# Fourteen of the last sixteen rows of v added by TensorE in two banks of its own, behind the first half's layers

## The reference

```
act = gelu(einsum("chkd,cd->chk", take(u, idx), xc))
out = einsum("chk,chkd->cd", act * gates, take(v, idx))
```

## Time and profile before

| | us |
|---|---|
| median of 3 runs | 2494.62 (2493.06 to 2494.7) |
| the profiled execution | 2490.55 |
| its span | 2488.8, so 1.75 outside |
| TensorE busy | 2112.2 (85%) |
| VectorE busy | 1832.5 (74%) |
| ScalarE busy | 1179.3 (47%) |
| GpSimd busy | 757.1 (30%) |
| gathers (q0) | 536.90 MB, 53.0% of the 16 engines' span |
| weights and stores (q1) | 222.15 MB, 23.5% |

### The profile page before, as it was taken

One profiled execution on the slowest core, in us unless ns is written; L12 is line 12 of the kernel. 1 busy time (PEld: TensorE's weight loads), 2 busy tenths in 40 slices (PEclk: granted clock), 3 DMA queues, 4 the chain that ended last, 5 costly groups with the idle time before them and its releaser, 6 DMA issues.

```text
span 2488.8 us, 28611 instructions
## 1 busy us (share of the span) xinstructions
PE 2112.2 (85%) x9508; PEld 1497.4 (60%) x9508; DVE 1832.5 (74%) x3372; ACT 1179.3 (47%) x3776; POOL 757.1 (30%) x634
## 2 busy tenths in 40 slices
PE   6987898988777777999675578699949999998999
PEld 6965443433222225884343466488429978898997
DVE  6985676868888887887898977776575646656564
ACT  5214555555666664442455654433244435435443
POOL 0001444454555553232465643333320001100000
PEclk9988899999999998999785689899969999999999
DMA  5111999999999999999998999999975543224453
GB/s 212 69 68 70 387 403 413 416 417 421 421 421 420 412 418 346 386 421 397 380 416 342 375 414 365 380 411 420 388 319 185 187 176 140 73 98 148 174 187 135
DMA packets 107460, 760.89 MB, mean 306 GB/s; under 512 B 12064, under 2 KB 12832, under 8 KB 16432
## 3 DMA queue, kind: packets, MB, share of 16 engines
q0 software_dynamic: 73728, 536.90, 53.0%
q1 hardware_dynamic: 33584, 222.15, 23.5%
HBM read 756.91 MB, written 2.10 MB: 305 GB/s over the span
## 4 chain that ended last, share of the span: by engine, by line
PE 42%; DVE 9%; DMA 4%; issue 3%; ACT 2%; POOL 1%; DVEq 0%; ACTq 0%; POOLq 0%
PE bank L578 42%; DVE resid L1039 4%; DMA pair<-in_uv,idx 4%; DVE pair L1695 2%; DVE half L1033 1%; DVE tmp L1033 0%; PE bank L996 0%; ACT half L1780 0%; POOL smalls L2328 0%; DVE smalls L1354 0%; POOL pair L2379 0%; ACT sigB L1780 0%; PE bank L870 0%; DVE smalls L1440 0%; ACT frow L1780 0%
## 5 line engine op out<-in xcount | busy, mean ns | idle before, releaser
L2379 POOL DMA_INDIRECT pair<-in_uv,idx x512 | 646.7, 1263 | 882.5 <-DVE resid L1039 552.9
L1780 ACT ACTIVATE smalls<-smalls 128x1 f32<-128x1 f32 x2058 | 540.3, 286 | 661.3 <-DVE smalls L1695 643.2
L1695 DVE CUSTOM_DVE_ANT_0 pair<-pair,hn 128x1024 f32<-128x1024 f32 x512 | 623.7, 1219 | 159.2 <-DMA pair<-in_uv,idx 157.4
L578 PE MATMUL bank<-pair,diag 128*128 128x512 f32 x928 | 457.1, 624 | 122.4 <-ACT diag L1780 121.8
L578 PEld LDWEIGHTS bank<-pair,diag 128*128 128x128 f32 x928 | 167.9, 194 | 392.3 <-ACT diag L1780 247.0
L578 PE MATMUL bank<-ft,raw 128*128 128x256 f32 x1664 | 373.1, 387 | 11.9 <-DVE ft L1033 11.9
L1039 DVE SCALAR_TENSOR_TENSOR resid<-pair,smalls,resid 128x1024 f32<-128x1024 f32 x280 | 358.1, 1279 | 0.9 <-DVE resid L1039 0.5
L578 PEld LDWEIGHTS bank<-ft,raw 128*128 128x128 f32 x1664 | 323.1, 195 | 57.7 <-issue 12.5
L1033 DVE TENSOR_TENSOR half<-raw,half 128x1024 fp32r<-128x1024 f32 (+1 forms) x204 | 235.5, 1194 | 136.0 <-ACT half L1780 136.0
L578 PE MATMUL bank<-ft_hi,half 128*128 128x256 f32 x1664 | 305.9, 285 | 7.4 <-DVE ft_lo L1033 4.1
L578 PEld LDWEIGHTS bank<-ft_hi,half 128*128 128x128 f32 x1664 | 260.8, 191 | 8.3 <-DVE ft_lo L1033 4.3
(11 more groups left out here) (280 smaller groups left out, 2743.0 us busy)
## 6 DMA issues: line engine op xcount, KB each, us to landing
raw<-in_wts SPq DMA_DIRECT2D x196, 1024.0 KB, 6.2
pair<-in_uv,idx POOLq DMA_INDIRECT x512, 11.1
raw<-in_wts SPq DMA_DIRECT2D x10, 512.0 KB, 6.1
raw<-in_wts SPq DMA_DIRECT2D x4, 720.0 KB, 6.9
resid<-in_x SPq DMA_DIRECT2D x4, 512.0 KB, 6.1
out<-resid SPq DMA_DIRECT2D x8, 256.0 KB, 6.0
raw<-in_wts SPq DMA_DIRECT2D x2, 768.0 KB, 6.4
rowt<-in_rows SPq DMA_DIRECT2D x1, 1076.0 KB, 12.3
```

The costliest lines, as they stand in the source:

```text
L578: return e.matmul(o, a, b, start=start, stop=stop)
L1695: e.tensor_tensor_reduce(b[:, 0:1024], b[:, 0:1024], HN[i // 128], 1.0, 0.0, ALU.mult, ALU.add, actv[:, i % 8:i % 8 + 1]).then_inc(dotted, 1)
L1780: return e.activation(o, i, f, **kw)
L2379: e.indirect_dma_start(pair[i % NPAIR], None, uv, bass.IndirectOffsetOnAxis(ap=idx[:, n % SLOTS, k:k + 1], axis=0)).then_inc(pairs_in[i % ...
```

## The change

`ON_PE` becomes true for rows 496 to 509 too. Their matmuls are not in TensorE's loop over rows, which now ends at 496: they stand between chain A and chain B, after the transposes of tile 2, which are taken out of chain B and put ahead of them (`tiles=(0,)`), while those of tile 3 stay in it. They use two mix banks of their own (4 and 5, a fourth mix use that the plan gets after chain A's last FFN), and eight `late_diag` tiles instead of `diag`, in space that chain A has left by then. VectorE leaves out the fourteen adds, takes the banks over after the last dot (`mixed_in(3, PAIRS - 2)`) with a wait on its own two writes, and then adds rows 510 and 511 as before. GpSimd's and ScalarE's waits by `row_used` turn from `added` to `v_used` for the fourteen rows by themselves.

```diff
--- before.py
+++ after.py
@@ -112,7 +112,8 @@
 
 
 
-ON_PE = [i < HALF + 8 and not (i < 128 and i % 4 == 3) for i in range(PAIRS)]
+LAST_ON_PE = 496
+ON_PE = [i < HALF + 8 and not (i < 128 and i % 4 == 3) or LAST_ON_PE <= i < PAIRS - 2 for i in range(PAIRS)]
 
 ROUTES, SLOTS = [], 16
 for _k in [1] * 8 + [2] * 8 + [1, 2, 1, 2, 1] + [0] * 11:
@@ -219,6 +220,8 @@
         for stage, n, us in (("br", 16, 1.8), ("wo", 4, 7.0)):
             p.ring(stage + x, n, us)
         ffn(2)
+        if x == "A":
+            p.add("mix", [4, 5], told=False)
     return p
 
 
@@ -466,6 +469,7 @@
         assert MISC + 512 + 1024 <= CHAIN and PAIR + 6144 <= LOW
 
         FTS = {"1": [FT2[0], ar("ft_early", LAYER + 10752, 8 * HALF, R).rearrange("p (k t) -> p k t", k=8)], "m": FT2, "2": FT2}
+        late_diag = [ar(f"late_diag{i}", LAYER + 12800 + P * i, P) for i in range(8)]
         nearly = [ar(f"nearly{i}", LAYER + 9728 + 512 * i, 512) for i in range(2)]
         rate_on = [rowt[:, P * i:P * i + P] for i in range(2)]
         RATE = {"1": rowt[:, HALF:2 * HALF], "2": rowt[:, HALF:2 * HALF], "m": ar("rate_m", LAYER + 14080, HALF)}
@@ -742,10 +746,10 @@
                     if begun:
                         fresh("mix", 2 * t + h)
                     b = B["mix", 2 * t + h]
-                    ins = mm(bank[b.bank][:], diag[i % 8], pair[i % NPAIR][:, 1024 + h * 512:1536 + h * 512], begun, done)
+                    ins = mm(bank[b.bank][:], (diag if i < LAST_ON_PE else late_diag)[i % 8], pair[i % NPAIR][:, 1024 + h * 512:1536 + h * 512], begun, done)
                 ins.then_inc(v_used, 1)
 
-            for i in range(PAIRS):
+            for i in range(LAST_ON_PE):
                 if i % 16 == 0:
                     steps = scores_in_steps(i // 16 + 2) if i < 128 else iter(())
                 if ON_PE[i]:
@@ -802,10 +806,10 @@
                 for n in range(4):
                     taken(e, "norm" + k if k[0] != "m" else "norm_" + k, n)
 
-            def turned_unscaled(k, from_):
+            def turned_unscaled(k, from_, tiles=(0, 1)):
 
                 stage = "norm" + k if k[0] != "m" else "norm_" + k
-                for i in range(2):
+                for i in tiles:
                     if from_ is not None:
                         taken(e, from_, i)
                         taken(e, from_, 2 + i)
@@ -832,7 +836,7 @@
                 if p == "A":
                     normed(f"{f}{p}")
                 else:
-                    turned_unscaled(f"{f}{p}", None if f == 1 else "wo" + p)
+                    turned_unscaled(f"{f}{p}", *((None, (1,)) if f == 1 else ("wo" + p,)))
                     e.wait_ge(ft_lo, 4 if f == 1 else 12)
                 ft, hidden = either(FT, FTS[str(f)], p), either(H, H2, p)
 
@@ -1019,6 +1023,9 @@
                         ins.then_inc(done, 1)
 
             chain("A")
+            turned_unscaled("1B", None, (0,))
+            for i in range(LAST_ON_PE, PAIRS - 2):
+                add_row(i)
             chain("B")
 
 
@@ -1751,6 +1758,9 @@
                         if k == 7:
                             final_row(n // 8 - 1)
                     first.until(clock(i))
+            mixed_in(3, PAIRS - 2)
+            for h in range(2):
+                taken(e, "mix", 6 + h)
             for i in (PAIRS - 2, PAIRS - 1):
                 add_row(i)
             first.until(1e9)
@@ -2273,7 +2283,7 @@
                         if i >= 8:
                             e.wait_ge(v_used, UP_TO[i - 7][0])
                         e.wait_ge(weighed, i + 1)
-                        act(diag[j], idt[:], ACT.Copy, scale=wgt[:, j:j + 1]).then_inc(diagd, 1)
+                        act((diag if i < LAST_ON_PE else late_diag)[j], idt[:], ACT.Copy, scale=wgt[:, j:j + 1]).then_inc(diagd, 1)
                     if k in (5, 9, 13, 14):
                         next(steps, None)
                     for x, r in enumerate(ROUTES[n]):
```

## The result

| | before | after |
|---|---|---|
| median of 22 runs each, side by side | 2493.28 (2489.03 to 2496.86) | 2497.16 (2491.93 to 2503.56) |
| the profiled execution, its span | 2490.55, 2488.8 | 2501.28, 2499.5 |
| start of the tile 2 transposes | 1825.16 | 1827.42 |
| start of the tile 3 transposes | 1859.83 | 1864.86 |
| between them ("the stretch") | 34.67 | 37.44 |

All in us. The ratio after to before is 1.0017, with a 95% interval of 1.001 to 1.0025: 2.5 to 6.2 us slower. Fourteen adds are gone from VectorE (busy time 14.1 less), and nothing of that reached the end. Only the stretch can be laid to the change instruction by instruction.

A forecast was written before the change was run, and what follows sets the result against it. VectorE and DMA, within 2 us of each other, bound the kernel: 14.0 us of adds removed, but DMA ends 2.9 later; with the tail, tile 3's transposes start +1.5 us. Added to 2494.62: 2496.1, range 2494.2 to 2498.2.

The forecast's parts named there:

- Adds removed: VectorE behind chain A: 12 of the 14 adds taken off were 14.0 us of work, the gross gain.
- TensorE's block: TensorE after the tile 2 transposes: rows 496 to 502 added back to back in 12.0 us, free since TensorE was idle.
- Release: Gather of row 503 waits for row 496's matmuls, issuing at 1828.3; nine gathers instead of seven follow chain A.
- The rate behind the hole: DMA engines after chain A: 5.0 us unused, 2.1 refilled by weights moving up, so row 511 lands 2.9 later.
- if none: Upper bound on the DMA delay: +5.0 us if no weights or stores move up into the unused time.
- Row 503's landing: First gather behind chain A: takes 6.5 us and lands at 1834.8, eight more following at 2.49 each.
- Tail: VectorE after row 511 lands: dot at about 1855.4, `mixed_in` 1.28, 0.4 for `taken`, two last adds, end 1861.3.
- `mixed_in` and TensorE: VectorE's wait for TensorE's row 509 at the end: matmuls done at 1855.1, 1.5 us before VectorE asks.
- rival (c): TensorE cools between rows 502 and 503 and `mixed_in` waits for it: 3.0 us more, 2501.2 in all; 12%.
- rival (b): TensorE keeps its clock over the 6 us before the tile 3 transposes: -3.7 us, 2492.4; 7%.
- rival (a): VectorE alone bounds the stretch and the gathers keep up: -12.3 us, 2482.3; 6%, with what lies between.
- The rest at nothing: Banks 4 and 5, `late_diag` and the first half's last store (about 2 later) were taken to cost nothing.

The follow-up runs named there:

- the repeat: The changed kernel run once more with nothing altered, before beside it: median 2494.08, ratio 1.0011 [1.0002, 1.002], stretch 37.57.
- experiment 1: Two kernels against the change: only rows 503 to 509 on TensorE (2495.04, ratio to before 1.000); the four stores five weight chunks later (2493.29, 1.0003).

## Why the prediction was right, and where it was off

The forecast was 1.5 us slower; the stretch says 2.6 to 2.8, the medians 3.9 (2.7 by the ratio of the repeat). The mechanism held: no gain, because the release of slots moves with the adds. That the forecast time, 2496.1, lies only 1.1 from the 2497.16 measured is in part luck: it started from 2494.62, the median of 3 runs, and 22 runs put before at 2493.28. It also took 5 us for the least that can be told from nothing; with 22 runs each the interval, 2.5 to 6.2 us, leaves zero out.

- **Adds removed.** 14.1 us of VectorE's busy time went, all of it hidden. The experiments with light gathers and with rows from 500 show that it was worth something otherwise.
- **TensorE's block.** Seven rows in 12.18, predicted 12.0; it waited for nothing there.
- **Release.** The gather of row 503 went 3.03 after the start of the transposes of tile 2 (1827.42 to 1830.45), predicted 3.1, and that of row 502 long before, at 1808.50.
- **The rate behind the hole: the mis-sized term.** The weights moved up into the hole as forecast: in the 13 us that answer to the earlier trace rows, 1816.3 to 1829.3, q1 moved 2.42 MB, where 1.61 + 0.9 = 2.5 was taken and before had 1.61. But all that follows the hole was taken at 421 GB/s, and the slices 1829 to 1838 moved 254, 339 and 386, which falls short of 421 by (167 + 82 + 35) x 3 / 421 = 2.0 us of transfers. Row 511 landed at 1859.5 (12.7 after its issue), 32.1 behind the tile 2 transposes, where before has 27.0: +5.1 against a forecast of +2.9, the far end of its bounds, and not for the reason that they gave ("if none" moves up).
- **Row 503's landing, the same seen forward.** Predicted 6.5, by the row of 6.6 "when little else was queued"; measured 8.6, 2.1 more. The slow weights and then the stores were queued ahead of it. With the stores gone it is 6.39 to the dot, although the rate is still low (363 and 350). After row 503 the spacing was as taken: dot 511 at 1859.58 is 20.5 behind dot 503, and 8 x 2.49 + 0.6 = 20.5. In all, dot 511 came 32.2 after the tile 2 transposes, 1.9 more than the 30.2 of the forecast (1825.16 to 1855.4).
- **Tail.** Dot 511 to the transposes took 5.28, predicted 5.95. The 0.4 for `taken` on itself isn't there: from `mixed_in` (1860.73 and 1.28) to the adds there is 0.1, and the two adds run together in 2.69 instead of 3.0. That was 0.7 too much. So two errors partly cancelled, 1.9 - 0.7 = 1.2: the stretch was forecast at 36.2 (1825.16 to 1861.35) and came out at 37.44.
- **`mixed_in` and TensorE, rival (c).** Row 509 was done at 1859.6, 1.1 before VectorE began (1.5 predicted), and the granted clock was 1.00 through all rows: between rows TensorE stood for 0.5 to 1.6 only. Row 503 was used at 1839.11, before TensorE was through with 502 (1840.5): the idleness that (c) needs was 1.6 us, not 2.5.
- **Clock kept, rival (b).** It fell again, to 0.51 in 1862 to 1865. It rose earlier against chain B's first product than before, 3.3 us after it instead of 5.6; before's own repeat has 5.4, after's 3.0, and other kernels with moved rows have 3.0 to 5.9, so it is not settled by the change alone.
- **VectorE alone, rival (a).** It needs a stretch of 22.4 (34.67 - 12.3). With the gathers at half their bytes the change still took 30.91, and no kernel here came under 29.78.
- **The rest at nothing.** The bank waits and `late_diag` show no new wait. SP's stores were in this list ("go about 2 later"). It asked when they go, not what stands behind them: experiment 1 puts their place ahead of the last gathers at 2.7 us of the stretch.

## What to carry to other kernels

Whoever moves the use of a ring's slot to another engine moves its release: look where that engine is in its program order when the slot used to come free, and count the transfers that then go behind it. The rows to move are those whose slots are released late anyway (here not 496 and 497); with that and the stores out of the way a loss of 3.9 us became a gain of about 5. When a hole opens in DMA time, ask which queued transfers will fall into it and whether an urgent one stands right behind them; stores that nobody waits for belong behind the last gather.

## What the runs showed of the hardware

- The busy share of the DMA engines is not the rate. Full slices moved 254 GB/s (share 0.99, weights alone), 350 (1.00, gathers alone) and 418 to 421 (1.00 to 1.02). The low ones came in the 12 us behind a slice in which the engines had run partly empty (share 0.34 in after, 0.64 in the change with later stores); in the slowest slice a packet of 8 KB took 0.51 us, in full ones at 421 GB/s 0.31. The cause is not shown.
- Four stores of 0.26 MB in packets of 2 KB cost about 2.8 us of the DMA engines, and 2.7 us of the stretch when they stood ahead of the last gathers.
- A gather's time does not scale with its bytes: with the stores ahead of it row 503 took 8.66 us from issue to dot for 1.05 MB and 6.89 for 0.52 MB, and without them 6.39 for 1.05 MB.
- The same instructions took 624.1 to 632.7 us in fourteen profiled executions of nearly the same program: after a pause of TensorE of 2 us the clock was at 1.2 GHz for 10 to 14 us in five, for at most 3.5 in nine. One profile of each kernel would have put 6 us of that down to the change.
